# Partial router sums in four column tiles, and expert 0's tokens gathered in f32

## What is computed

```python
h = rmsnorm(x, norm_ffn_g)
logits = (xt @ w_router + b_router).astype(jnp.float32)   # 256 x 32
top_vals, top_idx = lax.top_k(logits, TOP_K)              # 4 of 32 experts
gates = jax.nn.softmax(top_vals, axis=-1)
...
gu = xb @ w1[e] + b1[e]                                   # tokens of expert e
gate = jnp.minimum(gu[:, :F], SWIGLU_LIMIT)
up = jnp.clip(gu[:, F:], -SWIGLU_LIMIT, SWIGLU_LIMIT)
act = (up + 1.0) * gate * jax.nn.sigmoid(SWIGLU_ALPHA * gate)
return act @ w2[e] + b2[e]
```

## Time and profile before

| | us |
|---|---|
| median of 3 runs | 1223.25 |
| lowest, highest | 1222.76, 1223.86 |
| profiled execution, its device time | 1222.69 |
| span of its instructions | 1220.6 |
| TensorE busy | 1165.6 |
| VectorE, ScalarE, GpSimd busy | 420.0, 206.7, 59.5 |

### The profile page before, as it was taken

How to read it: one execution, slowest core, us unless ns; L and a number is a source line. 1 busy time by engine, 2 the same in 40 slices (tenths; PEclk the granted TensorE clock), 3 DMA queues, 4 the chain that set the end, 5 groups by cost and what they waited for, 6 DMA issues and landing times.

```text
span 1220.6 us, 17008 instructions
## 1 busy us (share of the span) xinstructions
PE 1165.6 (95%) x7179; PEld 586.5 (48%) x7179; DVE 420.0 (34%) x741; ACT 206.7 (17%) x305; POOL 59.5 (5%) x43
## 2 busy tenths in 40 slices
PE   9999999999999999999999999999998999999897
PEld 8888888888633343333333333333333333333332
DVE  5676764665732223222222222222222222222222
ACT  6444553534400000000000000000000000000001
POOL 0860000000300000000000000000000000000000
PEclk9999999999999999999999999999999999999999
DMA  9756437877899999999999999999999999999996
GB/s 314 270 207 221 158 138 257 320 285 313 340 429 428 433 432 432 430 428 431 431 433 432 432 433 431 432 431 433 433 432 432 433 431 432 432 433 432 432 421 261
DMA packets 46537, 462.42 MB, mean 379 GB/s; under 512 B 3745, under 2 KB 5730, under 8 KB 31170
## 3 DMA queue, kind: packets, MB, share of 16 engines
q1 hardware_dynamic: 43784, 459.49, 90.4%
q10 hardware_dynamic: 2714, 2.35, 0.7%
HBM read 459.71 MB, written 1.07 MB: 377 GB/s over the span
## 4 chain that ended last, share of the span: by engine, by line
PE 66%; DMA 33%; DVE 1%; ACT 0%; issue 0%; SPq 0%; DVEq 0%; ACTq 0%
DMA w_ring<-in_w 19%; PE ps L1314 19%; PE ps L1381 12%; DMA A_QK<-in_w 6%; DMA xb_and_att<-in_w 6%; PE ps L1031 4%; PE ps L1470 4%; PE ps L1039 3%; PE ps L1037 3%; PE ps L1038 3%; PE ps L1288 2%; PE ps L1032 2%; PE ps L1051 1%; PE ps L1164 1%; PE ps L1166 1%; PE ps L1165 1%
## 5 line engine op out<-in xcount | busy, mean ns | idle before, releaser
L1314 PE MATMUL ps<-w_ring,A_W 128*64 128x512 f32 x1216 | 272.4, 595 | 26.8 <-DMA w_ring<-in_w 26.8
L1907 DVE TENSOR_SCALAR A_W<-ps 128x512 f32<-128x512 f32 x32 | 22.1, 691 | 477.1 <-PE ps L1314 477.1
L1314 PEld LDWEIGHTS ps<-w_ring,A_W 128*64 128x64 f32 x1216 | 85.7, 137 | 198.7 <-issue 167.6
L1381 PE MATMUL ps<-w_ring,A_W 128*64 128x512 f32 x576 | 130.6, 595 | 0.0
L1551 DVE TENSOR_TENSOR w_parts<-w_ring,w_parts 128x1024 fp32r<-128x1024 f32 x76 | 101.7, 1350 | 60.8 <-ACT w_parts L758 59.9
L1314 PE MATMUL ps<-A_QK,A_W 128*64 128x512 f32 x416 | 93.2, 595 | 9.8 <-DMA A_QK<-in_w 9.8
L939 ACT ACTIVATE A_W<-ps 128x512 f32<-128x512 f32 x31 | 18.5, 597 | 459.0 <-PE ps L1362 459.0
L1314 PE MATMUL ps<-xb_and_att,A_W 128*64 128x512 f32 x368 | 82.7, 596 | 9.4 <-DMA xb_and_att<-in_w 9.4
L758 ACT ACTIVATE w_parts<-w_ring 128x1024 fp32r<-128x1024 f32 x75 | 78.9, 1058 | 64.7 <-PE ps L1032 32.1
L935 ACT ACTIVATE A_W<-A_W 128x512 f32<-128x512 f32 x32 | 20.2, 631 | 366.1 <-DVE A_W L1907 366.1
L1031 PE MATMUL ps<-hT_both,w_parts 128*128 128x512 f32 x224 | 79.3, 399 | 0.0
(11 more groups left out here) (265 smaller groups left out, 1207.5 us busy)
## 6 DMA issues: line engine op xcount, KB each, us to landing
w_ring<-in_w SPq DMA_DIRECT2D x47, 4096.0 KB
A_QK<-in_w SPq DMA_DIRECT2D x16, 4096.0 KB
xb_and_att<-in_w SPq DMA_DIRECT2D x16, 4096.0 KB
w_ring<-in_w_in SPq DMA_DIRECT2D x36, 1024.0 KB, 7.3
w_ring<-in_w SPq DMA_DIRECT2D x16, 2048.0 KB, 39.5
A_QK<-in_w SPq DMA_DIRECT2D x4, 2048.0 KB
xb_and_att<-in_w SPq DMA_DIRECT2D x3, 2048.0 KB
w_ring<-in_w SPq DMA_DIRECT2D x6, 1024.0 KB, 37.0
```

The lines of the kernel that those rows point to most:

```text
L1314: mm = pe.matmul(o, x[:, k, :], hidden_columns(tile[:, j, :], c), start=(k == 0), stop=(k == KC - 1))
L1381: mm = pe.matmul(ps[CAP * c:CAP * c + CAP, 3, :], lhs, w2_tile(flat)[:, q % W2_ROWS, c * HALF:(c + 1) * HALF], start=False, stop=(q == FQ ...
L1907: dve.tensor_scalar(gl, bank(b), LIMIT, None, ALU.min).then_inc(s.g, 1)
```

## The change

The diff, cut to its core, with "..." where lines are left out:

```diff
-            def logits(t, ks):
+            def partial_logits(t, ks):
                 for k in ks:
-                    rows = wr_sb[:, k, :].rearrange("p (a e) -> p a e", a=1).broadcast_to([P, 4, N_EXP])
-                    mm = pe.matmul(ps[:, t, 0:P].rearrange("p (a e) -> p a e", a=4), xT[t][:, k, :], rows,
-                                   start=(k == 0), stop=(k == KC - 1))
+                    g = k % 4 * N_EXP
+                    mm = pe.matmul(ps[g:g + N_EXP, t, 0:P], wr_sb[:, k, :], xT[t][:, k, :], start=(k < 4), stop=(k >= 4))
                 return mm
+
+            def logits(t):
+                pe.wait_ge(s_lgs[t], 1)
+                pe.matmul(ps[:, t, 0:N_EXP], partial[t], stacked[:, :], start=True, stop=True).then_inc(s_lg, 1)
...
+            squares(0)
             for h in range(2):
                 act.wait_ge(s_xt, h + 1)
                 act.activation(xT[0][:, 4 * h:4 * h + 4, :].rearrange("p k q -> p (k q)"), bank(h), ACT.Copy)\
                     .then_inc(s_xte, 1)
+            root(0)
+            act.wait_ge(s_lgp, 1)
+            act.activation(partial[0], ps[:, 0, 0:P], ACT.Copy).then_inc(s_lgs[0], 1)
+            squares(1)
+            root(1)
             high_part(2)
-            root_mean_square(0)
             high_part(3)
             middle_part(2)
-            root_mean_square(1)
+            high_part(0)
             middle_part(3)
+            high_part(1)
...
+            dve.wait_ge(s_lgp, 2)
+            dve.tensor_copy(partial[1], ps[:, 1, 0:P]).then_inc(s_lgs[1], 1)
...
-                link(dve.max_index(ids[:, t, :].bitcast(U32), best[:, t, :], lg[t]))
...
-                link(dve.tensor_tensor(chosen[:, t], experts, owners, ALU.is_equal))
-                dve.tensor_reduce(mask_bf[:, t, :], chosen[:, t].rearrange("p j e -> p e j"), AX.X, ALU.max).then_inc(s_mask, 1)
+                row = top[:, 8 * t:8 * t + TOP_K]
+                wanted = bass.AP(row.tensor, row.offset, [row.ap[0], [108, 2], [1, TOP_K]])
+                link(dve.match_replace(emptied[:, t, :], wanted, lg[t], -NO_LOGIT))
+                dve.tensor_scalar(mask_bf[:, t, :], emptied[:, t, :], -NO_LOGIT, None, ALU.is_equal).then_inc(s_mask, 1)
...
-            dve.tensor_scalar(s_onef, slot_ids[:, 0:CAP], posm[:, 0, 0:1], None, ALU.is_equal).then_inc(s_slots0, 1)
-            residual_scale(1)
+            dve.tensor_scalar(s_onef, slot_ids[:, 0:CAP], posm[:, 0, 0:1], rstd[:, 0:1], ALU.is_equal, ALU.mult)\
+                .then_inc(s_slots0, 1)
             choose_experts(1)
             positions(1)
-            dve.tensor_scalar(s_one[:, 1, :], slot_ids[:, 0:CAP], posm[:, 1, 0:1], None, ALU.is_equal)\
+            dve.tensor_scalar(s_onef1, slot_ids[:, 0:CAP], posm[:, 1, 0:1], rstd[:, 1:2], ALU.is_equal, ALU.mult)\
                 .then_inc(main.slots, 1)
...
+            def gather_first(t, ks):
+                for k in ks:
+                    b = 3 if k < 2 else 2 if k < 4 else 0
+                    mm = pe.matmul(ps[:, b, k * CAP:(k + 1) * CAP], row_columns(x2[:, t, :], k), s_onef1 if t else s_onef,
+                                   start=(t == 0 and k in (0, 2, 4)), stop=(t == 1), skip_group_check=True)
+                return mm
...
+            pe.wait_ge(main.slots, 1)
+            gather_first(1, range(2)).then_inc(s_gfirst, 1)
+            fill(FIRST_BANK, 4)
...
+                def gather_rest(u):
+                    if u < 2:
+                        gather_first(1, range(4 * u, 4 * u + 4) if u else range(2, 4)).then_inc(main.gathered, 1)
+
                 for u in range(W1_UNITS):
                     pe.wait_ge(s_unit[u], 16)
-                    if u == 1:
-                        pe.wait_ge(main.x, 1)
-                    hidden_unit(first_units[u], u, s_wu, FIRST_BANK, XT_first).then_inc(s_used, 1)
+                    pe.wait_ge(*((s_xfirst, u + 1) if u < 2 else (main.x, 1)))
+                    hidden_unit(first_units[u], u, s_wu, FIRST_BANK, XT_first, lambda: gather_rest(u)).then_inc(s_used, 1)
...
+            def store_first(b, rows):
+                return dve.tensor_tensor(XT_first[:, rows, :], bank(b).rearrange("p (k s) -> p k s", k=KC)[:, rows, :],
+                                         gain_of_row[:, rows, :], ALU.mult)
+
+            dve.wait_ge(s_gfirst, 1)
+            store_first(3, slice(0, 2)).then_inc(s_xfirst, 1)
             dve.wait_ge(main.gathered, 1)
...
+            store_first(2, slice(2, 4)).then_inc(s_xfirst, 1)
             choose_bias(sel1, main.sel1, 0)
             choose_bias(sel2, main.sel2, 0)
...
             slots(main, 1, 1)
+            dve.wait_ge(main.gathered, 2)
+            store_first(0, slice(4, KC)).then_inc(main.x, 1)
```

More of the change, by code:

```diff
@@ L31 @@
 MASKED = -1.0e30
+NO_LOGIT = 3.0e38
 RH = 4
@@ L104, in host_constants @@
     item = np.tile((P - np.arange(P, dtype=f)), (1, 1))
-    e_of = np.tile(np.arange(N_EXP, dtype=f), (P, 1))
     return {"c_early": early, "c_lasting": lasting, "c_decay": decay, "c_onehot": onehot,
-            "c_mask": mask, "c_item": item, "c_expert": e_of}
+            "c_mask": mask, "c_item": item}
 def hybrid_block_kernel(nc, x_in, g_mix, w_in, rel_bias, w_att, w_ret, w_out, g_ffn, w_router, b_router,
                         w1, b1, w2, b2, g_final, c_early, c_lasting, c_decay, c_onehot, c_mask, c_item,
-                        c_expert, out):
+                        out):
     with ExitStack() as ctx:
@@ L209, in hybrid_block_kernel @@
         top = route[:, 0:128]
+        partial = [A_W[:, 5120 + P * t:5120 + P * (t + 1)] for t in range(TT)]
+        s_onef1 = A_W[:, 5760:5760 + CAP]
         gates = route[:, 128:192].rearrange("p (t c) -> p t c", t=TT)
@@ L336, in hybrid_block_kernel @@
         s_lg = sem("logits_done")
+        s_lgp = sem("logit_partial_sums_done")
+        s_lgs = [sem(f"logit_partial_sums_stored{t}") for t in range(TT)]
+        s_gfirst = sem("first_rows_of_first_tokens_gathered")
         s_tk = sem("top_values_ready")
@@ L893, in high_part, with squares @@
                 t, h, cols = HALVES[n]
[L894 removed]
                 act.activation(x_part(0, t)[:, cols], x2[:, t, cols], ACT.Copy).then_inc(s_hi, 1)
[L897 removed]
+            def squares(t):
+                act.wait_ge(s_x2, 2 * t + 2)
                 act.activation(bank(4, 2), x2[:, t, :], ACT.Square, accum_out=ssq2[:, t:t + 1]).then_inc(s_sq, 1)
[L899 to L901 removed]
             def middle_part(n):
@@ L908, in _, with root @@
             act.activation(warm, warm, ACT.Sqrt)
-            high_part(0)
-            high_part(1)
+            def root(t):
+                act.wait_ge(s_sq, TT + t + 1)
+                act.activation(rstd[:, t:t + 1], ssq2[:, t:t + 1], ACT.Sqrt, bias=eps_col, scale=1.0 / D)\
+                    .then_inc(s_root, 1)
+            squares(0)
             for h in range(2):
@@ L1290, in gather, with hidden_unit @@
                 mm.then_inc(s.gathered, 1)
-            def gather_first():
-                pe.wait_ge(main.slots, 1)
-                for part, (ready, count) in enumerate(((s_hi, 2 * TT), (s_mid, 2), (s_lo, 2))):
-                    pe.wait_ge(ready, count)
-                    for k in range(KC):
-                        mm = pe.matmul(ps[:, 2, k * CAP:(k + 1) * CAP], row_columns(x_part(part, 1), k),
-                                       s_one[:, 1, :], start=False, stop=(part == 2), skip_group_check=True)
-                    if part == 0:
-                        pe.wait_ge(s_rsp, 4)
-                        for n in range(3):
-                            scales = pe.matmul(ps[:, 3, 0:CAP], rs_parts[:, n, 1:2].broadcast_to([P, P]), s_one[:, 1, :],
-                                               start=False, stop=(n == 2), skip_group_check=True)
-                        scales.then_inc(main.gathered, 1)
-                mm.then_inc(main.gathered, 1)
-            def hidden_unit(flat, u, row_done=None, b=0, x=XT):
+            def hidden_unit(flat, u, row_done=None, b=0, x=XT, second_row=None):
                 tile = w1_tile(flat)
@@ L1311, in hidden_unit @@
                     k = u * W1_ROWS + j
+                    if j and second_row is not None:
+                        second_row()
                     for c in range(4):
@@ L1700, in _ @@
                 low(u)
-            dve.wait_ge(s_small, 80)
+            link(dve.memset(top[:, 108:120], NO_LOGIT))
+            dve.wait_ge(s_ident, 16)
+            dve.tensor_reduce(stacked[:, :], ident.rearrange("p (a e) -> p e a", a=4), AX.X, ALU.add).then_inc(s_wr, 1)
+            dve.wait_ge(s_small, 64)
             for k in range(KC):
```

76 lines of the change are left out of this document (25 added, 51 removed).

## The result

The changed kernel takes 1224.73 us (median of 20 runs, 1223.18 to 1226.86), the kernel before beside it 1222.89 (20 runs, 1222.30 to 1223.86). The ratio is 1.0014, with a 95% interval of 1.0008 to 1.0021: slower by 1.8 us, and outside the forecast range of 1221.5 to 1224.4. The profiled execution took 1224.88 us against 1222.69.

A forecast was written before the change was run, and what follows sets the result against it. The expert weight stream bounds the kernel, from its last break at 320 to 322 us. First row 0.5 us sooner, plus 0.1 for the ramp, gave -0.4: 1222.3 profiled, 1222.8 median, range 1221.5 to 1224.4.

The forecast's parts named there:

- the rival of the clock: Router wait: TensorE's clock falls to 1.2 GHz, expert 0's rows take twice 1.8 us at first; 1225 to 1226, chance 0.04.
- the gathers between the weight rows: Expert 0's first units: six products of tile 1 between weight rows add 1.6 us of TensorE work, charged at 0.1.
- the ramp: Weight stream restarting behind the break: the second weight row brings data slightly late, charged at 0.1 us.
- cover at the seventh issue: Weight stream at 334.01 us: data already issued still covers the later TensorE, with 0.4 us left.
- sooner by S does give S back: Start of the unbroken weight stream: starting S earlier shortens the time by S until the break closes; S forecast 0.5 us.
- Column tiles: Router logits: a token tile's partial products take 0.7 us, between 0.47 with four overlapping and 1.87 with none.
- Mask: Choosing experts: one operation of 0.2 us replaces comparison and reduction; tile 0's mask at 313.8, ahead of GpSimd by 0.35.
- The rival in which GpSimd comes first: Router: GpSimd takes the shared port before the first mask, which waits out a whole subtraction; time 1224.0, chance 0.20.
- Holds: Router: VectorE's slot and mask steps wait for GpSimd's running subtractions; slots 315.25, second mask 316.45, second slots 317.6.
- The rival without a hold: Router: GpSimd does not hold VectorE's mask and slot steps; first row 1.3 us sooner, time 1222.0, chance 0.20.
- The break: Gap in the weight stream near 320 to 322 us, worth 2.9; closed by a start before 317.5: 1220.4, chance 0.02.
- the signs that would make me wrong: Products over 1 us, first mask after 315, stream break before 334, clock under 1.00, third unit waiting for a store.

The follow-up runs named there:

- e1: Changed kernel with more idle TensorE products (nine and sixteen instead of six and six, three new ones between the first gathers and the second mask's wait): 1222.28 us.
- e8: Kernel of e3 with the gathers of tile 1's rows 2 to 7 moved ahead of expert 0's first weight row: 1221.98 us.
- e9: Kernel before with its eighteen idle products cut from 128 columns to 32, same number of instructions: 1222.89 us.
- e11: Kernel of e3 with tile 1's rows 2 and 3 gathered ahead of the first weight row, rows 4 to 7 between rows: 1221.23 us.
- e2: Changed kernel with GpSimd's subtractions of the rests made to wait for tile 1's slots: 1221.90 us.
- e3: Changed kernel with nine, nine and three idle products and GpSimd's rests behind tile 1's slots: 1221.43 us.
- e5: Changed kernel with the logits of both tiles as in the kernel before, the column tiles undone: 1222.65 us.
- e6: Changed kernel with the old warm-up of 81 products of 72 columns put back: 1225.03 us.
- e10: Kernel of e2 with its sixteen idle products cut from 128 columns to 32, same number of instructions: 1224.12 us.
- e4: Kernel before with its three groups of six idle TensorE products taken out: 1232.32 us.
- e7: Changed kernel with GpSimd's rests behind tile 1's slots and all sixteen idle products taken out: 1231.25 us.
- e12: Kernel of e3 with the old mask (index search, comparison, reduction) and fifteen, nine and nine idle products: 1229.94 us.

## Why the prediction was wrong

**The step that failed is the rival of the clock.** It was in the text, with nearly the right time (1225 to 1226), and got a chance of 0.04 because the granted clock is 1.00 in the rows of before. Those rows are of a program whose TensorE worked through the router: 3.51 us of logits, f32 gathers, eighteen idle products. The change takes most of the logits away, and my own sum said when TensorE would have nothing left: partial sums done at 312.2, mask at 313.8, slots at 315.25. I worked out these times for VectorE's sake and did not add up what they leave TensorE to do. So the sum had the clock at nothing and the first weight row at 1.8 us. Measured, TensorE was busy 0.92 of 2 us from 314, and from 317 it ran at 1.2 GHz for 6.8 us; the row took 3.68, and SP's first issue came at 322.90 instead of 320.9. The price: 2.45 us (after to e1).

**A second term was too small: the gathers between the weight rows.** I charged 0.1 us for the ramp and counted on 0.4 us of cover at the seventh issue. At 75 MiB the lag is still the shift of the first issue, within 0.12 us in every kernel: there, sooner by S does give S back. What is lost is lost behind it. How far the seventh issue falls behind against the first, and what the lag loses from 75 to 430 MiB, shows it:

- e8 and e9: 0.0 us each, losses 0.11 and 0.36.
- e11: (333.80 - 334.01) - (319.97 - 321.42) = 1.24, loss 0.65.
- e1, e2, e3, e5, e6, e10: 2.0 each, losses 0.78, 0.84, 0.94, 0.83, 0.77, 0.63.
- after: 3.91 - 1.48 = 2.43, loss 1.01.

So a microsecond costs some 0.3, beside the 0.1 to 0.4 that are lost with no delay at all, and no cover within which it is free is to be seen. Why it is a part and not all or nothing stays open.

The delay itself was 2.0 where I had 1.6 (1.1 and the 0.5 of the stream), 0.13 for each of twelve records. TensorE in e1, from the first gathers between rows on:

```profile
320.49 0.69 PE L1272 MATMUL ps<-A_W 128*128 128x64 f32 x4
321.10 1.94 PE L1314 MATMUL ps<-A_ATT,A_W 128*64 128x512 f32 x8
...
324.69 1.16 PE L1272 MATMUL ps<-A_W 128*128 128x64 f32 x8
325.77 0.65 PE L1314 MATMUL ps<-w_ring,A_W 128*64 128x512 f32 x2
```

Four records take 0.61 us up to the next row, eight 1.08: 0.118 for one more. But e1's second issue comes 2.49 us behind the first instead of 1.71, and the fourth 2.95 behind the third instead of 1.72: 0.78 for four records, 1.23 for eight. So each break between weight rows costs some 0.3 us besides its records, and 12 x 0.118 + 2 x 0.3 = 2.0; e11, with one break of eight, has 0.94 + 0.3 = 1.24, as measured. The rows use half-width tiles (128*64), the gathers full-width ones (128*128). That the switch is what costs 0.3 is argued, not shown.

Without the fall of the clock this loss and an earlier first issue (320.59 for 320.9) cancel: for the profiled execution I had 1222.3, and e1's took 1222.31. That close a hit is luck, and e1's interval against the kernel before, 0.9985 to 1.0003, includes 1: with the clock held, the change alone is not shown to be faster.

**The other steps.**
- Column tiles: no more than 0.67 us a token tile (1.34 for two) against 0.7 of 0.47 to 1.87. The row of 1.34 holds a wait for VectorE's second copy as well. By the single records, tile 0 starts at 310.59 and tile 1 at 311.11: 0.52 us, near the 0.47 of four tiles that overlap fully. The last transpose starts 0.21 us ahead of the first of them, where one transpose follows another by 0.12: if the switch to column tiles costs anything here, it is about 0.1 us. The logits operation came at 312.40, 0.4 earlier than I had.
- Mask: 0.18 us against 0.2; ahead of GpSimd by 0.29 against 0.35. The rival in which GpSimd comes first did not happen.
- Holds: slots 0 to 314.87, mask 1 to 315.98, slots 1 to 317.11, against 315.25, 316.45 and 317.6: 0.4 to 0.5 earlier throughout, as the chain began earlier. The rival without a hold is ruled out by e2.
- Start of the first row: 318.95 forecast, 319.19 measured; 318.62 in e1. The five gathers and the two rows of tile 1 at the lower clock took the lead away.
- SP's first issue: 320.9 forecast, 320.59 in e1, 322.90 in the changed kernel. I set the time by the start of the first row; what counts is its end, and the two part when the clock falls.
- The break: a start before 317.5 would not have closed it. A gain of 2.9 us on 319.45 needs 316.55, and e3, which starts at 317.71, still shows 201 GB/s instead of some 431 at 320 to 322 us.
- Of the signs that would make me wrong, two appeared: a granted clock under 1.00, and a thinner stream before 334 us.

## What to carry to other kernels

Before taking work from TensorE, or making it wait, ahead of the products that everything waits for, add up its busy time stretch by stretch in the new order; a stage in which it was covered by slow code may be what keeps its clock. Sixteen more idle products in the gaps were worth 2.45 us here. And where a break in a stream is to be closed early by moving work behind it, look at the later issues as well: 1.40 us at the first issue were worth 0.55. Work put between two weight rows cost some 0.3 us for each break, besides its own time.

## What the runs showed of the hardware

The clock can fall in some executions of a program and not in others (e2: six runs near 1221.6 us at a mean granted clock of 0.998 to 0.999, four near 1224.0 at 0.996 to 0.997), so one profile doesn't show whether a kernel is safe; the spread of its runs does.

Some sixteen to eighteen products more or fewer ahead of the expert loop went with a cost far above their own: e4, e7 and e12 have 67 instruction transfers where the other kernels have 31, and all three lose 3.6 to 3.7 us between 150 and 430 MiB, and more behind that. In e12 the clock is 1.00 in the router, so the loss goes with the transfers and not with the fall there. What makes a kernel one of 67 is not shown: e1, with sixteen products more, has 31. TensorE's wait without a cause came to 2.63 and 3.16 us near 601 us in e4. (0.59 MB more in 36 transfers is 16.4 KB each. The Trainium skill, "Advanced Engine Details and Errata", ISA Cache, says that instructions are cached in lines of 16 KB; the size agrees. That the loop no longer fits is only argued from it; no run here shows which program's lines were fetched again.)
